# Other starting positions for the low parts of split weights, one for each stretch of the program

## The chip, the core and the metric

The kernel runs on one core of a Trainium2 chip. The metric is the device time of one execution in microseconds (us), as the median of several runs; lower is better. Beside it stands one profiled execution, whose span (first to last instruction) the traces are read against.

## What is computed

The reference is a small encoder of two layers on x (256 positions, 2048 features, float32). Cut to what matters here:

```python
xn = _rmsnorm(x, norm_gain[0])
q, k, v, gate = split(xn @ attn_w_in)          # 2048 x 8192
a = softmax(q1 k1 + bias) - lam * softmax(q2 k2 + bias)
x = x + (norm(a @ v) * silu(gate)) @ attn_w_out    # 2048 x 2048
xn = _rmsnorm(x, norm_gain[1])
a, g, z = split(xn @ conv_w_in + b)            # 2048 x 6144
u = layernorm(depthwise_conv31(a * sigmoid(g)))
x = x + (silu(u) * silu(z)) @ conv_w_out + b   # 2048 x 2048
return _rmsnorm(x, final_gain)
```

Nearly all work is in the four products with weights: 18432 columns of 2048 weights each.

## The kernel before

**The split.** A product of float32 operands is made of three products in float32r, a format that TensorE takes in one pass but rounds. Each operand is split in a high part (rounded) and a low part (the rest), and high times high, high times low and low times high are added up in PSUM.

**The ring of weights.** The weights pass in 144 chunks of 4 x 128 rows by 512 columns (1 MiB), through a ring of four slots. A DMA on SP's queue brings a chunk to `w_raw[slot]`; ScalarE writes the high part to `w_hi[slot]` (`high_part`, L463); VectorE (`low_part`, L807), or GpSimd in the middle of the second layer and for one chunk before it (L435), writes `w_lo[slot]`; TensorE multiplies and counts up `w_free`, which lets ScalarE write the slot again. All four steps of a chunk are released by semaphores.

**Two kinds of chunk.** In a *turned* chunk the weights are the stationary operand and 256 columns of activations stream past them (`project_tile`): 48 matmuls of 128x256 in a chunk, 16 of them with a low part as the stationary operand (L1238, in the first four chunks L1284). Q and K of the attention and all of the conv input are turned: 80 chunks. In a *rows* chunk the activations are stationary and 512 columns of weights stream (`project`): 24 matmuls of 128x512 in a chunk, 8 of them with the low part moving (L1223). V, the gate and both output products are rows: 64 chunks. In the profile's names the moving operand of a matmul stands first and the stationary one second.

**The places in a slot.** Each slot of `w_hi` and `w_lo` is 2048 elements and a gap of `W_GAP` = 128 (8704 bytes, 17 times 512). A chunk's part begins at an offset in its slot, the same for high and low: 0 for a turned chunk, 16 elements for a rows chunk (`place`, L296). Every reader and writer takes its view from `w_part` (L306), with the same chunk number. Within a chunk the pieces lie 512 or 2048 bytes apart. By the program's allocation all slots of `w_hi` and `w_lo` begin 128 bytes past a multiple of 512 bytes in their partition, and the activations (`act_hi`, `act_lo`, `conv_hi`, `conv_lo`) and the small operands q, k, v 192 bytes past one; their own pieces lie multiples of 512 bytes apart. So, modulo 512 bytes, a turned weight lies at 128 and the activations that stream past it at 192; a moving rows weight lies at 192 (128 + 64), as its stationary activations do.

**Order.** The attention runs in four pairs of heads (pair 0, a hardware loop over pairs 1 and 2, pair 3), each with four chunks of Q, K, V and gate. The scores (L1310 to L1312) and the product with V (L1324 to L1326) stand between rows chunks. Then come 16 chunks of output product, 48 turned chunks of the second layer's input, and 16 rows chunks of its output. In the 48, VectorE computes the convolution's taps (L1039), and after each pair of tiles TensorE does four transposes (`v_turn`, L1197) of `uT`, whose rows are 1144 bytes apart.

Of the kernel before, what the change touches and what calls it, by code (L numbers as in the profile page):

```python
# [37 lines left out]
NCH = KT // CK  # L38
# [6 lines left out]
CHUNKS_ATT = 4 * NCH * PAIRS  # L45
CHUNKS_OUT = CHUNKS_ATT + NCH * PAIRS
CHUNKS_CONV = CHUNKS_OUT + 3 * NCH * PAIRS
# [3 lines left out]
VEC_ROOM = 9 * KT + 4  # L51
W_GAP = 128
TURNED_AT, ROWS_AT = 0, 16
WARM_UP = 9
POOL_FROM = CHUNKS_OUT + 2 * RING
POOL_TO = CHUNKS_CONV + RING
# [16 lines left out]
def build(nc, x, x_turned, vectors, taps, final_gain, rel_bias, attn_w_in, attn_w_out, conv_w_in,  # L73
          conv_w_out, conv_b_out, out):
    with ExitStack() as ctx:
        def sb(name, shape, dt=F32, scope=ctx):
            return scope.enter_context(nc.sbuf_tensor("sb_" + name, shape, dt))
# [10 lines left out]
        w_hi = [sb(f"w_hi{i}", [P, CK * GW + W_GAP], F32R) for i in range(RING)]  # L88
# [165 lines left out]
        at = 0  # L254
        for i in range(CONV_START, CONV_END + 1):
            upto = len(STEPS) * (i + 1 - CONV_START) // (CONV_END + 1 - CONV_START)
            steps_at[i] = STEPS[at:upto]
            at = upto
# [37 lines left out]
        def place(c):  # L296

            turned = c % 16 < 2 * NCH if c < CHUNKS_ATT else CHUNKS_OUT <= c < CHUNKS_CONV
            return TURNED_AT if turned else ROWS_AT

        def pair_chunk(j, i):

            in_loop = type(j) is not int
            return 16 * (1 if in_loop else j) + i

        def w_part(parts, c):  # L306

            at = place(c)
            return parts[c % RING][:, at:at + CK * GW].rearrange("p (k n) -> p k n", k=CK)

        def low_part_ready(eng, c):
# [99 lines left out]
        def _(pool):  # L411
# [20 lines left out]
            def low_part(c):  # L432

                pool.wait_ge(hi_ready, c + 1)
                pool.tensor_tensor(w_part(w_lo, c), w_raw[c % RING][:], w_part(w_hi, c).bitcast(F32),  # L435
                                   ALU.subtract).then_inc(lo_ready_pool, 1)
# [22 lines left out]
        def _(act):  # L459
            def high_part(c, slot, loads, like=None):  # L460
                act.wait_ge(landed[slot], 16 * loads)
                act.wait_ge(w_free, c + 1)
                act.activation(w_part(w_hi, c if like is None else like), w_raw[slot][:], ACT.Copy  # L463
                               ).then_inc(hi_ready, 1)
# [14 lines left out]
            for p, (k0, k1) in enumerate(HEAD):  # L479
                slot, rows, closes = head_piece(p)  # L480
                act.wait_ge(x_landed[p], 16)
                for kt in range(k0, k1):
                    act.activation(act_hi[:, kt], xT[:, kt], ACT.Copy, scale=gain_in[:, kt:kt + 1]
                                   ).then_inc(split_hi, 1)
                if p:
                    act.wait_ge(piece_landed(p), 16)
                    act.activation(w_part(w_hi, slot)[:, rows], w_raw[slot][:, rows], ACT.Copy
                                   ).then_inc(hi_ready if closes else head_hi, 1)
# [35 lines left out]
            def pair_slot(j, i):  # L524

                G, A = 4 * j, A_START + A_PER_PAIR * j
                if i in (9, 10):
                    high_part(16 * j + i + RING, i % NCH, 4 * j + i // NCH + 2, pair_chunk(j, i + RING))
                    for hq in ((0, 1) if i == 9 else (2, 3)):
                        act.wait_ge(max_ready, 4 * j + hq + 1)  # L530
                        for c in range(2):
                            act.activation(probs[:, hq, c], probs[:, hq, c], ACT.Exp,
                                           bias=neg_max[:, 2 * hq + c:2 * hq + c + 1],
                                           accum_out=row_sum[:, 2 * hq + c:2 * hq + c + 1]
                                           ).then_inc(exp_done, 1)
                    return
# [34 lines left out]
                if i == 15:  # L571
                    empty_acc(G + 3, 1, g_rows, ACT.Silu, rstd)
                high_part(16 * j + i + RING, i % NCH, 4 * j + i // NCH + 2, pair_chunk(j, i + RING))

            def m_high(n):
# [219 lines left out]
        def _(dve):  # L795
# [61 lines left out]
            def pair_slot(j, i):  # L857
# [84 lines left out]
                if not by_pool(16 * j + i + RING):  # L942
                    low_part(16 * j + i + RING, i % NCH, pair_chunk(j, i + RING))
# [251 lines left out]
        def _(pe):  # L1195
# [133 lines left out]
            pe.wait_ge(consts_ready, 1)  # L1329
            for _ in range(WARM_UP):  # L1330
                pe.matmul(bank_d[0][:, 0:P], ones[:], ones[:], start=True, stop=True)
# [109 lines left out]
```

## Time and profile before

| | |
|---|---|
| median of 3 runs | 842.39 us (841.7 to 846.05) |
| the profiled execution, its own time | 841.85 us |
| its span | 840.1 us |
| TensorE busy | 830.6 us, 5628 matmuls |
| VectorE busy | 646.6 us |
| ScalarE busy | 448.9 us |
| GpSimd busy | 226.4 us |

The profiled execution's time is 1.75 us more than its span (what lies around it), and 0.54 us under the median. Ends of matmuls are modelled in these profiles: a matmul shows a longer duration than the distance to the next one, and the distance is what costs time. It is read from a stretch's length and the number of matmuls in it.

### The profile page before, as it was taken

What the parts mean: (1) busy time and instruction counts of PE and PEld (TensorE: products, weight loads), DVE (VectorE), ACT (ScalarE), POOL (GpSimd) and SP (SyncE); (2) the same over time, 40 slices, a digit from 0 to 9 for tenths busy, and PEclk for the clock granted to TensorE, in tenths of its full rate; (3) what the DMA queues carried; (4) which work ended last, traced back from release to release, by engine and by line L of the source; (5) the groups of instructions that cost most, each with busy time, mean ns of one, the idle gap of its engine ahead of it and who ended that gap; (6) DMA issues with size and microseconds to landing.
All of it is one profiled execution on the core that took longest, in us unless ns stands there. A gap on an engine that the chain in (4) does not pass through costs nothing.

```text
span 840.1 us, 13845 instructions
## 1 busy us (share of the span) xinstructions
PE 830.6 (99%) x5628; PEld 769.4 (92%) x5628; DVE 646.6 (77%) x1097; ACT 448.9 (53%) x589; POOL 226.4 (27%) x107
## 2 busy tenths in 40 slices
PE   9999999999999999999999999999999999999996
PEld 9998899889998899888888999999999999998885
DVE  7569784697658784698788978999999997566651
ACT  7756643646336643556544464454555456594432
POOL 0200000000000000002000008888889877680000
PEclk9999999999999999999999999999999999999998
DMA  9977566546654566534655665555555655549502
GB/s 327 395 275 265 170 200 202 181 139 200 208 192 150 169 199 203 184 117 158 228 181 188 199 211 191 189 171 193 199 163 192 200 173 180 189 163 350 183 18 100
DMA packets 99649, 163.68 MB, mean 195 GB/s; under 512 B 3584, under 2 KB 40704, under 8 KB 99080
## 3 DMA queue, kind: packets, MB, share of 16 engines
q1 hardware_dynamic: 98112, 160.64, 56.4%
q10 hardware_dynamic: 1480, 2.25, 0.7%
q8 instruction: 39, 0.64, 0.3%
q14 instruction: 18, 0.15, 0.1%
HBM read 160.76 MB, written 3.69 MB: 196 GB/s over the span
## 4 chain that ended last, share of the span: by engine, by line
PE 96%; SPq 2%; DMA 1%; ACT 1%; DVE 0%; issue 0%; ACTq 0%
PE ps_acc L1238 17%; PE ps_acc L1237 17%; PE ps_acc L1235 17%; PE ps_acc L1221 14%; PE ps_acc L1223 14%; PE ps_acc L1224 14%; SPq L345 1%; DMA sb_w_raw<-in_attn_w_in 1%; SPq L344 1%; PE ps_d L1312 0%; PE ps_a L1326 0%; PE ps_a L1325 0%; PE ps_d L1311 0%; PE ps_a L1324 0%; PE ps_d L1310 0%; PE ps_a L1197 0%
## 5 line engine op out<-in xcount | busy, mean ns | idle before, releaser
L463 ACT ACTIVATE sb_w_hi<-sb_w_raw 128x2048 fp32r<-128x2048 f32 x140 | 267.1, 1916 | 244.3 <-PE ps_acc L1238 168.2
L435 POOL TENSOR_TENSOR sb_w_lo<-sb_w_raw,sb_w_hi 128x2048 fp32r<-128x2048 f32 x45 | 208.6, 4642 | 404.7 <-ACT sb_w_hi L463 404.7
L807 DVE TENSOR_TENSOR sb_w_lo<-sb_w_raw,sb_w_hi 128x2048 fp32r<-128x2048 f32 x95 | 216.2, 2289 | 98.7 <-ACT sb_w_hi L463 98.3
L1235 PE MATMUL ps_acc<-sb_conv_hi,sb_w_hi 128*128 128x256 f32 x768 | 214.9, 280 | 0.0
L1237 PE MATMUL ps_acc<-sb_conv_lo,sb_w_hi 128*128 128x256 f32 x768 | 213.9, 278 | 0.0
L1238 PE MATMUL ps_acc<-sb_conv_hi,sb_w_lo 128*128 128x256 f32 x768 | 213.7, 278 | 0.0
L1039 DVE SCALAR_TENSOR_TENSOR ps_d<-sb_uT,sb_dwT,ps_d 128x256 f32<-128x256 f32 x480 | 188.9, 481 | 4.5 <-ACT ps_d L688 4.5
L1221 PE MATMUL ps_acc<-sb_w_hi,sb_act_hi 128*128 128x512 f32 x384 | 149.7, 390 | 0.0
L1223 PE MATMUL ps_acc<-sb_w_lo,sb_act_hi 128*128 128x512 f32 x384 | 149.5, 389 | 0.0
L1224 PE MATMUL ps_acc<-sb_w_hi,sb_act_lo 128*128 128x512 f32 x384 | 149.4, 389 | 0.0
L1235 PEld LDWEIGHTS ps_acc<-sb_conv_hi,sb_w_hi 128*128 128x128 f32 x768 | 144.2, 188 | 0.1
L1237 PEld LDWEIGHTS ps_acc<-sb_conv_lo,sb_w_hi 128*128 128x128 f32 x768 | 144.1, 188 | 0.1
L1238 PEld LDWEIGHTS ps_acc<-sb_conv_hi,sb_w_lo 128*128 128x128 f32 x768 | 144.0, 188 | 0.0
L1235 PE MATMUL ps_acc<-sb_act_hi,sb_w_hi 128*128 128x256 f32 x448 | 125.1, 279 | 1.7 <-DVE sb_w_lo L807 1.7
L1238 PE MATMUL ps_acc<-sb_act_hi,sb_w_lo 128*128 128x256 f32 x448 | 125.2, 280 | 0.0
L1237 PE MATMUL ps_acc<-sb_act_lo,sb_w_hi 128*128 128x256 f32 x448 | 124.9, 279 | 0.0
L1224 PEld LDWEIGHTS ps_acc<-sb_w_hi,sb_act_lo 128*128 128x128 f32 x384 | 72.1, 188 | 15.1
L1221 PEld LDWEIGHTS ps_acc<-sb_w_hi,sb_act_hi 128*128 128x128 f32 x384 | 72.1, 188 | 14.8 <-DVE sb_act_lo L973 0.2
L1235 PEld LDWEIGHTS ps_acc<-sb_act_hi,sb_w_hi 128*128 128x128 f32 x448 | 83.8, 187 | 2.0 <-issue 1.9
L1223 PEld LDWEIGHTS ps_acc<-sb_w_lo,sb_act_hi 128*128 128x128 f32 x384 | 72.1, 188 | 14.2
L1237 PEld LDWEIGHTS ps_acc<-sb_act_lo,sb_w_hi 128*128 128x128 f32 x448 | 84.2, 188 | 0.1
L1238 PEld LDWEIGHTS ps_acc<-sb_act_hi,sb_w_lo 128*128 128x128 f32 x448 | 84.1, 188 | 0.0
(168 smaller groups left out, 874.2 us busy)
## 6 DMA issues: line engine op xcount, KB each, us to landing
sb_w_raw<-in_attn_w_in SPq DMA_DIRECT2D x60, 1024.0 KB, 5.6
sb_w_raw<-in_conv_w_in SPq DMA_DIRECT2D x64, 512.0 KB, 4.5
sb_w_raw<-in_attn_w_out SPq DMA_DIRECT2D x16, 1024.0 KB, 5.0
sb_w_raw<-in_conv_w_in SPq DMA_DIRECT2D x16, 1024.0 KB, 5.0
sb_w_raw<-in_conv_w_out SPq DMA_DIRECT2D x16, 1024.0 KB, 5.0
sb_w_raw<-in_attn_w_in SPq DMA_DIRECT2D x16, 256.0 KB, 4.5
sb_xs<-in_x SPq DMA_DIRECT2D x2, 1024.0 KB, 13.9
sb_x_in<-in_x_turned SPq DMA_DIRECT2D x15, 128.0 KB, 4.3
```

What stands on the lines that cost most here:

```text
L344: sp.dma_start(x_piece(x_in, p), x_piece(x_turned, p)).then_inc(x_landed[p], 16)
L345: sp.dma_start(w_raw[slot][:, rows], w_in[:, k0:k1, 0:GW]).then_inc(piece_landed(p), 16)
L435: pool.tensor_tensor(w_part(w_lo, c), w_raw[c % RING][:], w_part(w_hi, c).bitcast(F32), ALU.subtract).then_inc(lo_ready_pool, 1)
L463: act.activation(w_part(w_hi, c if like is None else like), w_raw[slot][:], ACT.Copy).then_inc(hi_ready, 1)
L807: dve.tensor_tensor(w_part(w_lo, like), w_raw[slot][:], w_part(w_hi, like).bitcast(F32), ALU.subtract).then_inc(lo_ready, 1)
L1039: dve.scalar_tensor_tensor(out_, uT[:, k, tap:tap + SEQ], dwT[:, k, tap:tap + 1], out_, ALU.mult, ALU.add).then_inc(tap_done, 1)
L1221: pe.matmul(into, left_hi, high[:, k], start=(kt == 0 and not filled), stop=False, skip_group_check=filled)
L1223: pe.matmul(into, left_hi, low[:, k], start=False, stop=False, skip_group_check=filled)
L1224: ins = pe.matmul(into, left_lo, high[:, k], start=False, stop=(kt == KT - 1), skip_group_check=filled)
L1235: pe.matmul(into, left_hi, hi[:, kt], start=(kt == 0 and f % 2 == 0), stop=False, skip_group_check=True)
L1237: pe.matmul(into, left_hi, lo[:, kt], start=False, stop=False, skip_group_check=True)
L1238: ins = pe.matmul(into, left_lo, hi[:, kt], start=False, stop=(kt == KT - 1), skip_group_check=True)
```

## The change

The low part of a chunk gets its own offset (`low_place`), while the high part keeps the one it had. The offset of the low part, in elements of 4 bytes, depends on the stretch: in turned chunks 16 for pair 0, 32 for Q and K of pairs 1 and 2 and Q of pair 3, 48 for K of pair 3; in rows chunks of the pairs 0, 32, 32 and 48; in the output product 8; in the 48 chunks of the conv input, eight by eight, 16, 32, 48, 8, 4 and 24; in the last output product 24. All lie within the gap that the slots have. Nothing is added, removed or moved in any engine's order; only the views that L435, L807, L839, L1223, L1238 and L1284 write or read differ.

```diff
 TURNED_AT, ROWS_AT = 0, 16
+LOW_TURNED_AT, LOW_ROWS_AT = (16, 32, 32, 48), (0, 32, 32, 48)
+LOW_OUT_AT, LOW_CONV_AT, LOW_CONV_OUT_AT = 8, (16, 32, 48, 8, 4, 24), 24
...
+        def low_place(c):
+
+            if c >= CHUNKS_CONV:
+                return LOW_CONV_OUT_AT
+            if c >= CHUNKS_OUT:
+                return LOW_CONV_AT[(c - CHUNKS_OUT) // (2 * NCH)]
+            if c >= CHUNKS_ATT:
+                return LOW_OUT_AT
+            j, t = c // 16, c % 16 // NCH
+            if t == 0 and j:
+                return LOW_TURNED_AT[1]
+            return LOW_TURNED_AT[j] if t < 2 else LOW_ROWS_AT[j]
...
         def w_part(parts, c):
 
-            at = place(c)
+            at = place(c) if parts is w_hi else low_place(c)
             return parts[c % RING][:, at:at + CK * GW].rearrange("p (k n) -> p k n", k=CK)
```

## Rows read from the trace of the kernel before

**Rows 1.** The page: TensorE's busy time, and its granted clock in 40 slices.

```profile
PE 830.6 (99%) x5628; PEld 769.4 (92%) x5628; DVE 646.6 (77%) x1097; ACT 448.9 (53%) x589; POOL 226.4 (27%) x107
PEclk9999999999999999999999999999999999999998
```

**Rows 2.** The page: the chain that ended last, by engine.

```profile
PE 96%; SPq 2%; DMA 1%; ACT 1%; DVE 0%; issue 0%; ACTq 0%
```

**Rows 3.** Waits: who waited for whom, us, times, longest.

```profile
ACT sb_w_hi L463 <- PE ps_acc L1238: 168.2, 60, 3.9
...
PE ps_acc L1235 <- DVE sb_w_lo L807: 1.7, 1, 1.7
```

**Rows 4.** Windows of turned chunks, L1235 alone (a third of the matmuls), first kind.

```profile
101.90:147.10 45.20, 35.66 (x128) 23.75 (x127) 1.00 0.59 194
...
472.70:546.80 74.10, 58.23 (x208) 38.87 (x207) 1.00 0.63 207
569.40:620.80 51.40, 40.43 (x144) 27.05 (x144) 1.00 0.56 185
648.80:718.00 69.20, 54.02 (x192) 36.07 (x192) 1.00 0.57 186
```

**Rows 5.** The same, second kind: window, length, matmuls and weight loads of L1235.

```profile
30.00:46.30 16.30, 13.28 (x48) 8.99 (x48) 1.00 1.00 373
547.20:569.00 21.80, 17.74 (x64) 12.01 (x64) 1.00 0.57 188
621.20:648.40 27.20, 22.14 (x80) 14.99 (x80) 1.00 0.56 181
718.80:746.10 27.30, 22.24 (x80) 14.96 (x80) 1.00 0.44 150
```

**Rows 6.** Windows of the first four chunks, L1277 alone (a third of the matmuls).

```profile
6.93:22.43 15.50, 6.94 (x44) 5.81 (x44) 1.00 1.05 375
...
24.03:26.75 2.72, 1.23 (x8) 1.05 (x9) 1.00 1.08 413
```

**Rows 7.** A window of the output product, L1221 alone (a third of the matmuls).

```profile
385.60:472.60 87.00, 49.87 (x128) 23.84 (x127) 1.00 0.53 180
```

**Rows 8.** Timeline of TensorE in the scores: start, us, line.

```profile
63.50 0.28 PE L1311 MATMUL ps_d<-sb_k_lo,sb_q_hi 128*128 128x256 f32 x1
...
64.70 0.28 PE L1312 MATMUL ps_d<-sb_k_hi,sb_q_lo 128*128 128x256 f32 x1
```

**Rows 9.** Timeline of TensorE behind the first two groups of transposes.

```profile
547.22 0.36 PE L1235 MATMUL ps_acc<-sb_conv_hi,sb_w_hi 128*128 128x256 f32 x1
547.42 0.28 PE L1237 MATMUL ps_acc<-sb_conv_lo,sb_w_hi 128*128 128x256 f32 x1
...
569.43 0.36 PE L1235 MATMUL ps_acc<-sb_conv_hi,sb_w_hi 128*128 128x256 f32 x1
569.64 0.28 PE L1237 MATMUL ps_acc<-sb_conv_lo,sb_w_hi 128*128 128x256 f32 x1
```

**Rows 10.** Weight loads of the transposes: min, median, max ns.

```profile
L1197 PEld LDWEIGHTS ps_a<-sb_ident,sb_uT x32: 137/140/143, 546.8 to 712.2; 128*128 128x128 f32 x32
```

**Rows 11.** The writers of the low parts: min, median, max ns of one.

```profile
L807 DVE TENSOR_TENSOR sb_w_lo<-sb_w_raw,sb_w_hi x95: 2277/2292/2294, 27.6 to 813.7; 128x2048 fp32r<-128x2048 f32 x95
...
L435 POOL TENSOR_TENSOR sb_w_lo<-sb_w_raw,sb_w_hi x45: 4617/4642/4690, 392.4 to 751.5; 128x2048 fp32r<-128x2048 f32 x45
```

**Rows 12.** A window of VectorE alone, to the end of the convolution's last tap.

```profile
520.00:710.30 190.30, 185.84 (x465) 1.00 0.57 186
```

**Rows 13.** Timeline where the convolution ends: last taps, then ScalarE's copy of them.

```profile
701.65 8.70 DVE L1039 SCALAR_TENSOR_TENSOR ps_d<-sb_uT,sb_dwT,ps_d 128x256 f32<-128x256 f32 x22
...
710.39 0.60 ACT L700 ACTIVATE sb_uT<-ps_d 128x512 f32<-128x512 f32 x1 [1.87 <-DVE ps_d L1039]
```

## The prediction

> **What bounds the kernel now.** I read the page first. TensorE is busy for 830.6 of 840.1 us and its granted clock stands in the highest tenth in all slices but the last [rows 1], which is the 2.4 GHz level. The chain that ended last is 96% TensorE [rows 2]. Then the waits: ScalarE waits 168.2 us for TensorE to free slots, while in the longest stretches TensorE waits for a low part once, for 1.7 us [rows 3]. So the supply of weights runs ahead, and the time is the sum of the distances between matmuls. An offset in SBUF adds no instruction; it can move the time only by changing these distances, or by slowing a writer so much that it falls behind.
>
> So I measured the distances, stretch by stretch, as length over matmuls (three times the count of one line). The turned chunks have two. In the first kind, 101.90 to 147.10 holds 3 x 128 matmuls: 45.2 / 384 = 117.7 ns. The stretches from 472.70, 569.40 and 648.80 give 118.8, 119.0 and 120.1 ns, with the pauses and transposes inside them [rows 4]; the Q and K stretches from 196.4 and 291.0 repeat the first row. In the second kind it is 113.2 ns (16.3 us for 144), 113.5, 113.3 and 113.8 [rows 5]. The first four chunks show both: 117.4 ns over 132 matmuls, then 2.72 us / 24 = 113.3 [rows 6]. Taking 117.78 and 113.33 as the two paces, 62 of the 80 turned chunks go at the slow one and 18 at the quick one. The rows chunks have one pace: 87.0 us / 384 = 226.6 ns [rows 7]. The scores, same shape as a turned matmul, go at (64.70 - 63.50) / 10 = 120 ns [rows 8].
>
> Streaming alone takes 256 / 2.4 GHz = 106.7 ns, or 213.3 for 512 columns. What is on top is 6.7, 11.1 or 13.3 ns. I work with 6.67 ns, the time of 16 columns or 64 bytes, as the quantum: quick turned matmuls have one, the scores and the rows matmuls two, the slow turned ones five in three matmuls.
>
> Do addresses matter to this? Two things speak on it. Chunks, slots and pieces move by multiples of 512 bytes and the pace of a stretch does not move with them, so only the place modulo 512 bytes can count. And scores and turned matmuls have the same shapes and the same order of high and low, but the scores' stationary and moving operands lie at the same place modulo 512 (192 and 192), as those of rows chunks do, while turned ones lie 64 bytes apart (128 and 192). The first two have two quanta everywhere, the turned ones one or one and two thirds. That is the only hint that place matters, and it is a correlation over two distances. Against it: at one and the same distance both turned paces occur, and which one a stretch gets is settled where it begins. After the first group of transposes the second matmul starts 0.20 us after the first and the stretch is quick; after the second group it is 0.21 us and the stretch is slow [rows 9, 5, 4].
>
> **The change part by part.** *The writers.* Every low part is written once more at another offset. VectorE needs 2277 to 2294 ns and GpSimd 4617 to 4690 ns whether the offset is 0 or 16 elements [rows 11]. Offsets 4, 8 and 24 are the first that are no multiple of 64 bytes. GpSimd is the one near a limit: a turned chunk lasts 48 x 117.78 = 5.65 us, so it has 1.0 us left; under 22% more per write costs nothing, and I take nothing for both. Beyond that, each of the 24 chunks of conv input at offsets 8, 4 and 24 would be late by the excess, and TensorE would wait for it.
>
> *Turned chunks, offset 16* (pair 0's Q and K and the first eight of the conv input: 16 chunks, 16 low matmuls each). The low weight comes to lie at 192, like the activations: the distance of the scores. Nearest row: 120 ns. 256 matmuls x 2.22 ns = +0.57 us. If the whole stretch goes to 120 from what it has, it is 12 x 48 x 2.22 + 4 x 48 x 6.67 = +2.6 us; if it goes to the quick pace, 12 x 0.213 = -2.6 us.
>
> *Turned chunks, offsets 32 and 48* (28 and 12 chunks). The low weight lies 64 and 128 bytes behind the activations; no row shows these distances. Bounds for a chunk: from 117.78 to 113.33, -0.213 us; to 120, +0.107 us. The high parts, two thirds of the loads, stay where they are, and I expect the stretch to keep its pace: 0.
>
> *Turned chunks, offsets 8, 4, 24* (24 chunks of the conv input). A stationary operand at no multiple of 64 bytes is shown by the transposes, whose tiles lie at steps of 1144 bytes: all 32 loads take 137 to 143 ns [rows 10]. So 0, with the same bounds.
>
> *Rows chunks.* In 16 (pairs 1 and 2, offset 32) the moving low weight gets 64 bytes away from the stationary operand, as in turned chunks; one matmul in three could have 2.2 ns less: 128 x 2.22 = -0.28 us. Pairs 0 and 3 (offsets 0 and 48): 0. The 32 chunks of the two output products (8 and 24) have a moving row of 2048 bytes that begins in the middle of 64 bytes and so touches 33 of them, not 32. A quantum for each would be 256 x 6.67 = +1.7 us, nothing if it hides in the two quanta already paid; no row decides, and I take half, +0.85 us. Bounds for all 512 low rows matmuls: a quantum less or more, -3.4 to +3.4 us.
>
> A rule of the Trainium skill speaks against any effect. SBUF — State Buffer, section "SBUF: two separate sides", has TensorE on ports of its own, with "2nd independent read port for LDWEIGHTS", and places its banks along partitions, not along a partition. By it the whole edit is worth 0 and the time is that of before; the rows neither confirm nor exclude it. TensorE: Matmul & The Clock Gate, section "Wait — 56ns, not 53.3ns?", gives streaming plus about 2.5 ns for a matmul, an estimate of 109.2 ns here; the rows disagree (113.3 to 120), so something is lost that this page does not explain.
>
> *Sum.* +0.57 - 0.28 + 0.85 = +1.1 us. On the profiled execution, 841.85 us (span 840.1 and 1.75 around it), it gives 842.95; on the median, 0.54 us higher, 843.5.
>
> **The rivals.**
>
> *Faster: the low parts release the slow pace.* If the slow pace is a lock between two equal streams, moving one load in three can break it. All 62 slow chunks at 113.33: 62 x 48 x 4.44 = -13.2 us, so 829.2 us; with half of it, 835.8. For it: the quick pace exists with the same instructions [rows 5]. Against: two thirds of the loads don't move. It would be given back in part in the second layer: VectorE has only 190.3 - 185.84 = 4.5 us idle up to its last tap [rows 12], and ScalarE's copy ends at 710.99 us [rows 13], about 1.0 us before the last four transposes, whose last load starts at 712.2 [rows 10], against 5.3 us that 25 slow chunks there would save. The cap of some 5.5 us just about lets it pass. I put it at 829 to 838.
>
> *Slower: every turned chunk goes at the pace of the scores.* One conflicting load in three upsets the other two, and the pace becomes 120 ns: 62 x 48 x 2.22 + 18 x 48 x 6.67 = 6.6 + 5.8 = +12.4 us, 854.8 us; with half, 848.6. Losing the quick stretches alone to 117.78 is 18 x 0.213 = +3.8 us. It decides against the kernel from 4.2 us, which a third of this sum reaches. For it: the only distances in the trace show equality as dearer, and unequal places of high and low put a jump into a stream that had none. With a quantum for each of the 512 rows matmuls too, 858.
>
> *Slower: a moving operand pays for the jump itself.* In rows chunks the stream goes high, low, high at one place now; if each jump costs a quantum, two in a triple, it is 512 x 2 x 6.67 = +6.8 us, 849.2 us. For it, rows chunks are so regular; against, turned ones don't change moving places and yet vary.
>
> *No effect of place at all*: 842.4, by the two separate reads. It falls together with my forecast. The draw of slow and quick stretches can still differ: one stretch of five chunks is 5 x 0.213 = 1.1 us.
>
> **How the numbers follow.** About 0.5%, 4.2 us, is what a measurement of this kernel can tell from no change. Chances: the forecast with the rival of no effect 0.38, near 843.5 (its own range 839 to 846.5, three or four stretches that change pace); the release 0.28, at 829 to 838; turned chunks at the scores' pace 0.24, at 847 to 855; the jump in rows 0.10, at 847 to 851. So faster 0.28, same 0.38, slower 0.34. The range is from 831, which leaves out the full release, to 855, the full loss.
>
> **What the profile after would show.** The distances by stretch: 113.3, 117.8 or 120 ns in the turned stretches, 226.7 or more in rows, above all in the output products with offsets 8 and 24. A distance outside these (say 115.6, or 240 and more) would say that place acts more strongly than by one quantum, and would make the sum wrong. The durations of L807 and L435 should stay at 2.29 and 4.64 us; waits of TensorE for L435 would mean that a writer suffers from the offset. If in one stretch the pace follows the offset and in none the beginning, place matters; if all stretches show the paces of before, it doesn't.

## The result and the profile after

The changed kernel takes 846.27 us (845.93 to 847.36, 10 runs) against 842.53 for the kernel before (10 runs): ratio 1.0044, 95% interval 1.0035 to 1.0052. It is slower by 2.9 to 4.4 us, less than 0.5% but clear of the noise. The forecast was a change within 0.5%, near 843.5 us, with an own range of 839 to 846.5: the measured time lies 2.8 us above the number and inside the range. Its profiled execution took 846.21 us (span 844.4), 4.36 more than the one of before.

The page after, busy times and granted clock, beside [rows 1]:

```profile
PE 835.2 (99%) x5628; PEld 767.5 (91%) x5628; DVE 646.2 (77%) x1097; ACT 449.2 (53%) x589; POOL 226.3 (27%) x107
PEclk9999999999999999999999999999999999999999
```

The same 5628 matmuls at the same clock keep TensorE busy 4.6 us longer. The writers did not change, whatever the offset (L822 and L450 are L807 and L435 of before, [rows 11]):

```profile
L822 DVE TENSOR_TENSOR sb_w_lo<-sb_w_raw,sb_w_hi x95: 2281/2291/2297, 27.1 to 817.6; 128x2048 fp32r<-128x2048 f32 x95
...
L450 POOL TENSOR_TENSOR sb_w_lo<-sb_w_raw,sb_w_hi x45: 4608/4634/4720, 392.6 to 753.1; 128x2048 fp32r<-128x2048 f32 x45
```

TensorE has no wait for either writer in the second layer. So it is the distance between matmuls again. Windows of rows chunks after, L1236 alone (a third of the matmuls; columns as in [rows 4]): three adjacent chunks each of pairs 0, 1 and 3, then the two output products.

```profile
77.54:94.04 16.50, 9.36 (x24) 4.32 (x23) 1.00 0.47 152
173.17:189.85 16.68, 9.45 (x24) 4.32 (x23) 1.00 0.46 149
361.13:377.78 16.65, 9.44 (x24) 4.31 (x23) 1.00 0.36 126
386.18:474.94 88.76, 49.99 (x128) 23.94 (x127) 1.00 0.53 182
748.62:832.03 83.41, 47.27 (x121) 22.61 (x121) 1.00 0.50 175
```

Length over three times the count: 229.2 ns with the low part at 0, 231.7 at 32, 231.3 at 48, 231.1 at 8, and 231.7 at 24 (83.41 us for the 15 chunks of 24 matmuls that end there). Before, all were at 226.7 [rows 7]. Every new offset made rows chunks dearer.

Windows of turned chunks after, L1250 alone: pair 1 and pair 2 (Q and K, offset 32), K of pair 3 (48), four chunks of the conv input (32) and its last four (24):

```profile
102.39:148.00 45.61, 35.72 (x128) 23.84 (x127) 1.00 0.57 190
198.32:241.80 43.48, 35.33 (x128) 23.84 (x127) 1.00 0.59 196
...
313.88:336.10 22.22, 17.85 (x64) 11.86 (x64) 1.00 0.67 224
...
520.60:542.36 21.76, 17.66 (x65) 12.01 (x65) 1.00 0.58 192
...
726.01:748.60 22.59, 17.92 (x64) 11.90 (x64) 1.00 0.46 152
```

All 24 chunks at 8, 4 and 24 ran at 117.7 to 118.0. Offset 32 gives 118.8 ns in pair 1 (45.61 / 384) and 113.2 in pair 2; 48 gives 115.7 (K of pair 3); the conv input has 21.76 / 192 = 113.3 at 32 and 117.7 at 24 in its last four chunks, which ran at 113.3 before. (A window's count can be one off at its ends; chunks are exact: 48 matmuls in each.) Summed over all matmuls by the distance to the next one, the rows stretches have 6.5 us more, the turned ones 2.0 us less and the rest 0.1 less: +4.4, the whole difference of the two executions.

### The profile page after: what moved, and what is told of

It is laid out like the page before. It is cut to its first block, busy times and chain, and to the rows that moved or that the text cites. A ratio compares the mean times of both kernels' runs of the same rounds, so it can differ in the third digit from the quotient of the medians.

```text
span 844.4 us, 13845 instructions
## 1 busy us (share of the span) xinstructions
PE 835.2 (99%) x5628; PEld 767.5 (91%) x5628; DVE 646.2 (77%) x1097; ACT 449.2 (53%) x589; POOL 226.3 (27%) x107
## 4 chain that ended last, share of the span: by engine, by line
PE 96%; SPq 2%; DMA 1%; ACT 1%; DVE 0%; issue 0%; ACTq 0%
PE ps_acc L1252 17%; PE ps_acc L1250 17%; PE ps_acc L1253 17%; PE ps_acc L1238 14%; PE ps_acc L1239 14%; PE ps_acc L1236 14%; SPq L360 1%; DMA sb_w_raw<-in_attn_w_in 1%; SPq L359 1%; PE ps_a L1341 0%; PE ps_a L1339 0%; PE ps_a L1340 0%; PE ps_d L1326 0%; PE ps_d L1327 0%; PE ps_d L1325 0%; PE ps_a L1212 0%
## 5 line engine op out<-in xcount | busy, mean ns | idle before, releaser
L450 POOL TENSOR_TENSOR sb_w_lo<-sb_w_raw,sb_w_hi 128x2048 fp32r<-128x2048 f32 x45 | 208.8, 4644 | 404.7 <-ACT sb_w_hi L478 404.7
L822 DVE TENSOR_TENSOR sb_w_lo<-sb_w_raw,sb_w_hi 128x2048 fp32r<-128x2048 f32 x95 | 216.1, 2290 | 101.5 <-ACT sb_w_hi L478 101.1
L1250 PE MATMUL ps_acc<-sb_conv_hi,sb_w_hi 128*128 128x256 f32 x768 | 214.9, 280 | 0.0
L1238 PE MATMUL ps_acc<-sb_w_lo,sb_act_hi 128*128 128x512 f32 x384 | 151.4, 394 | 0.0
L1239 PE MATMUL ps_acc<-sb_w_hi,sb_act_lo 128*128 128x512 f32 x384 | 151.1, 394 | 0.0
L1236 PE MATMUL ps_acc<-sb_w_hi,sb_act_hi 128*128 128x512 f32 x384 | 150.6, 392 | 0.0
L1250 PEld LDWEIGHTS ps_acc<-sb_conv_hi,sb_w_hi 128*128 128x128 f32 x768 | 144.3, 188 | 0.1
L1250 PE MATMUL ps_acc<-sb_act_hi,sb_w_hi 128*128 128x256 f32 x448 | 124.7, 278 | 1.4 <-DVE sb_w_lo L822 1.4
L1236 PEld LDWEIGHTS ps_acc<-sb_w_hi,sb_act_hi 128*128 128x128 f32 x384 | 72.2, 188 | 16.1
L1238 PEld LDWEIGHTS ps_acc<-sb_w_lo,sb_act_hi 128*128 128x128 f32 x384 | 72.1, 188 | 16.0
L1250 PEld LDWEIGHTS ps_acc<-sb_act_hi,sb_w_hi 128*128 128x128 f32 x448 | 84.1, 188 | 1.8 <-issue 1.6
```

The lines of the kernel that those rows point to most:

```text
L822: dve.tensor_tensor(w_part(w_lo, like), w_raw[slot][:], w_part(w_hi, like).bitcast(F32), ALU.subtract).then_inc(lo_ready, 1)
L1236: pe.matmul(into, left_hi, high[:, k], start=(kt == 0 and not filled), stop=False, skip_group_check=filled)
L1238: pe.matmul(into, left_hi, low[:, k], start=False, stop=False, skip_group_check=filled)
L1239: ins = pe.matmul(into, left_lo, high[:, k], start=False, stop=(kt == KT - 1), skip_group_check=filled)
L1250: pe.matmul(into, left_hi, hi[:, kt], start=(kt == 0 and f % 2 == 0), stop=False, skip_group_check=True)
```

## The experiments

All are the kernel before with other offsets. `place` takes them from two tables, for high and low parts, in the order of pair 0, pairs 1 and 2 (with Q of pair 3), pair 3, and the quarters of an output product or the twelve groups of four chunks of the conv input:

```diff
-        def place(c):
+        def place(c, part):
...
+            if c >= CHUNKS_CONV:
+                return ROWS[part][2][(c - CHUNKS_CONV) // NCH]
+            if c >= CHUNKS_OUT:
+                return TURNED[part][1][(c - CHUNKS_OUT) // NCH]
+            if c >= CHUNKS_ATT:
+                return ROWS[part][1][(c - CHUNKS_ATT) // NCH]
...
-            at = place(c)
+            at = place(c, 'hi' if parts is w_hi else 'lo')
```

In the profiles of these kernels L1231 and L1245 are L1221 and L1235 of before. "Alike" means high and low at the same offset.

**1. The rows' half alone.**

```diff
-ROWS low:  16 everywhere
+ROWS low:  0 | 32 | 48, output products 8 and 24
```

> The change in the rows chunks alone; low parts of turned chunks at 0 as before. If the place of a low part acts in its own chunks and nowhere else, the rows stretches show the distances of the changed kernel (229 to 232 ns) and give +6.5 us, with the turned stretches as before up to a redraw of their pace of 1 to 3 us: 847 to 851 us. If the dearer rows came from something shared (writers, the change of offset between stretches), they would be partly back at 226.7 ns and the time under 845.

844.62 us (10 runs; the kernel before beside it 842.59), ratio 1.0023 (1.0014 to 1.0033). Two windows of L1231, pair 1 and the first output product, then two of L1245, three chunks of K of pair 0 and Q and K of pair 2:

```profile
172.85:189.53 16.68, 9.45 (x24) 4.32 (x23) 1.00 0.47 149
385.42:474.17 88.75, 49.99 (x128) 23.91 (x127) 1.00 0.54 183
...
29.63:46.59 16.96, 13.46 (x48) 8.94 (x48) 1.00 1.01 375
198.01:241.53 43.52, 35.33 (x128) 23.84 (x127) 1.00 0.59 195
```

The two rows windows are those of the changed kernel to 0.01 us, and the rows stretches have +6.3 us in sum. (The last output product, at 24 in both, ran at 231.1 ns here and at 231.7 there: rows stretches can differ at one offset too.) But the turned chunks, in which nothing was edited, gained 3.6 us: pairs 2 and 3 went from 117.7 to 43.52 / 384 = 113.3 ns. The time came out 2.4 us under the expected range. By itself it would have fitted the rival of something shared (under 845); the distances of the rows, dearer throughout, refute that. So a turned stretch's pace hangs on more than its own offsets. Not only on the rows before it, either: K of pair 0, which runs before any rows chunk, went from 113.2 ns [rows 5] to 16.96 / 144 = 117.8.

**2. The turned half alone.**

```diff
-TURNED low:  0 everywhere
+TURNED low:  16 | 32 | 48, conv input 16, 32, 48, 8, 4, 24 (eight chunks each)
```

> The change in the turned chunks alone; low parts of rows chunks at 16 as before. Same theory: rows at 226.7 ns everywhere, turned at 113.3 ns where the low offset is 32, 115.6 where it is 48, 117.8 elsewhere: -2 us to -4 us, 838 to 841. Rival, that the pace of a turned stretch is drawn by how it begins and not by the offset: the paces by stretch then come in another order than in the changed kernel, 838 to 846.

838.02 us (4 runs), ratio 0.9944 (0.9924 to 0.9963). Windows of L1245, pair 1, K of pair 3 and the conv input at 32:

```profile
102.27:145.81 43.54, 35.33 (x128) 23.84 (x127) 1.00 0.62 204
309.82:331.98 22.16, 17.86 (x64) 11.87 (x64) 1.00 0.68 228
514.40:536.16 21.76, 17.66 (x64) 12.01 (x65) 1.00 0.59 192
```

Rows are at 226.7 again, turned chunks 4.0 us cheaper than before. Paces by offset are those of the changed kernel, except that pair 1 now has the quick one, 113.4 ns, at the same offset that gave 118.8 there. The change was two edits of opposite sign, and they don't add up: the halves alone are +2.0 and -4.6 us against the kernel before, -2.5 in sum, and the whole is +3.7. The rows' cost is the same with and without the other half (6.3 and 6.5 us); what differs are the turned chunks, 3.6 and 4.0 us cheaper in the halves and only 2.0 in the whole.

**3 and 4. Offset 32 in all turned chunks, low alone, and alike.**

```diff
-TURNED low:  0 everywhere
+TURNED low:  32 everywhere          (3: high 0, 4: high 32)
```

> Low parts at 32 in all turned chunks, rows as before. If offset 32 brings the quick pace, 62 slow chunks go from 117.78 to 113.33 ns: -13.2 us, 829 to 830. In the changed kernel Q and K of pair 1 ran at 118.9 ns at this offset; if the offset only makes the quick pace likelier, some stretches stay at 118 to 119: 831 to 840. If the pace is only drawn, 842 or so.

> High and low parts both at 32 in all turned chunks, rows as before. If what counts is where a stationary weight lies against the activations that stream (64 bytes ahead before, 64 bytes behind at 32), all three loads have now the place that only the low one had: the quick pace everywhere, 829 to 832. If it is the difference between high and low, there is none, as in the kernel before: paces mixed, 838 to 846.

Low alone: 837.39 us (6 runs), ratio 0.9946 (0.9926 to 0.9967). Alike: 839.80 us (7 runs), ratio 0.9959 (0.9945 to 0.9973). Two windows of L1245 of the first, pair 1 and three chunks of the conv input, then two of the second:

```profile
102.60:146.20 43.60, 35.33 (x128) 23.84 (x127) 1.00 0.61 200
546.60:563.70 17.10, 13.38 (x48) 8.89 (x48) 1.00 0.57 185
```

```profile
102.00:147.20 45.20, 35.97 (x128) 23.84 (x127) 1.00 0.59 197
...
655.70:672.00 16.30, 13.20 (x48) 8.85 (x48) 1.00 0.54 175
```

Low alone has 113.5 and 118.8 ns (17.10 / 144) and, behind the first three chunks, never 117.8. Alike has 117.7 and 113.2, as the kernel before, though the weights lie on the other side of the activations. Part of the first run's rival is what happened: the offset makes the quick pace likelier, and some stretches stay at 118 to 119 (831 to 840 us). "32 makes it quick" fell; so did my theory for the second run, that this side of the activations is the better one. What fits is that an offset sets which paces a stretch can have.

**5. Rows, high and low alike at other offsets.**

```diff
-ROWS high, low:  16 everywhere
+ROWS high, low:  0 | 32 | 48, first output product 0, 32, 64, 96, last 8, 24, 4, 16
```

> Turned chunks as before; in the rows chunks high and low parts lie at the same offset, but at another one in each stretch: 0, 32 and 48 in the pairs, 0, 32, 64 and 96 in the four quarters of the first output product, 8, 24, 4 and 16 in those of the last. If the difference between high and low makes rows dear, there is none: 226.7 ns everywhere, and 842 +- 2 us. If the place against the stationary activations does, 229 to 232 ns as in the changed kernel, 849. If a row that begins at no multiple of 64 bytes costs by itself, only 8, 24 and 4 are dearer (+2 us or so).

849.03 us (2 runs), ratio 1.0074 (1.0054 to 1.0094). L1231 in the four quarters of the first output product, then in those of the last (its last window holds three chunks of 24 matmuls):

```profile
389.24:411.64 22.40, 12.65 (x33) 6.02 (x32) 1.00 0.40 131
411.64:433.61 21.97, 12.42 (x32) 6.01 (x32) 1.00 0.60 216
433.61:456.00 22.39, 12.65 (x32) 6.02 (x32) 1.00 0.54 188
456.00:477.98 21.98, 12.42 (x32) 5.82 (x31) 1.00 0.59 191
751.20:773.61 22.41, 12.66 (x33) 6.09 (x33) 1.00 0.80 299
773.61:796.01 22.40, 12.64 (x33) 6.00 (x32) 1.00 0.66 227
796.01:818.53 22.52, 12.69 (x32) 6.03 (x32) 1.00 0.28 94
818.53:834.87 16.34, 9.34 (x25) 4.50 (x24) 1.00 0.14 54
```

By 96 matmuls to a quarter: 233.3, 228.9, 233.2, 229.0 ns, 233.4 at offset 8, 233.3 at 24, 234.6 at 4, and 226.9 at 16 in the end. Offset 32 has a second pace here: 228.9 ns in pair 1, but 233.3 from the second half of V of pair 2 to the end of that pair (16.80 / 72 in 268.38 to 285.18). No low part lies elsewhere than its high part, and all but 16 is dearer. The rival of the prediction that a jump of the moving stream costs is refuted as the cause: there is no jump in this run. And 64 equals 0, 96 equals 32: the period is 256 bytes, not only 512. Whether a row begins at a multiple of 64 bytes doesn't decide: 0 is as dear as 8. Offset 4 is the dearest of all by 1.3 ns; why, no run tells.

**6. A survey of differences between high and low.**

```diff
-TURNED low:  0 everywhere;  ROWS high, low:  16 everywhere
+TURNED low:  64 | 128 | 96 in the pairs, conv input 128, 64, 96, 112 (three groups each)
+ROWS high:  16 | 0 | 16, 16 16 16 0, 64 32 16 16;  low:  80 | 128 | 112, 0 32 80 128, 0 0 24 16
```

> A survey of differences low minus high, in elements. Turned: 64 for pair 0, 128 for pairs 1 and 2 and Q of pair 3, 96 for K of pair 3, and 128, 64, 96, 112 for three groups each of the conv input. Rows: 64, 128, 96 in the pairs, -16, 16, 64, 128 in the quarters of the first output product, -64, -32, 8, 0 in those of the last. If only the difference modulo 512 bytes counts, 128 equals 0: rows at 226.7 ns, turned at 113.3 or 117.8. If a smaller period holds (256 bytes), 64 is like 0 too. If the difference as such costs, 128 is as dear as 16 or 32 (229 to 232 ns). Time not forecast; the distances by stretch are what counts.

850.31 us (1 run). L1231 in three chunks of pair 0 (16 and 80), of pair 1 (0 and 128), and in the third and fourth quarter of the first output product (16 and 80, 0 and 128):

```profile
77.97:94.29 16.32, 9.34 (x24) 4.32 (x23) 1.00 0.49 154
173.13:189.93 16.80, 9.46 (x24) 4.31 (x23) 1.00 0.46 149
...
434.39:456.18 21.79, 12.47 (x33) 6.01 (x32) 1.00 0.55 190
456.18:478.57 22.39, 12.62 (x32) 5.80 (x31) 1.00 0.58 191
```

and L1245 in K of pair 3 (low at 96) and three of the last four chunks of the conv input (low at 112):

```profile
316.79:339.61 22.82, 17.88 (x64) 11.90 (x64) 1.00 0.62 205
...
730.98:747.62 16.64, 13.41 (x49) 8.99 (x49) 1.00 0.44 149
```

A low part 256 bytes behind the high one's place costs nothing (226.7 and 227.0 ns), and 512 bytes behind offset 0 it is as dear as 0 alike (233.3 and 233.2). So both of my cases for 128 failed as stated: the difference is without effect, but the base of it wasn't 226.7. In turned chunks 64 and 128 ran at 117.8, the slow pace of 0; 96 at 118.9 (four chunks of 16 at 113.3), as 32 did, and 112 at 115.6 (16.64 / 144), as 48 did. So the period of 256 bytes shows in turned chunks as well.

**7. The activations moved by 64 bytes, with rows alike.**

```diff
-        o_stat = sb("o_stat", [P, 16])
+        o_stat = sb("o_stat", [P, 32])[:, 0:16]
-ROWS high, low:  16 everywhere
+ROWS high, low:  16 | 32 | 48, first output product 32, 16, 0, 80, last 32
```

> All activations moved by 64 bytes (o_stat made 16 elements longer), turned weights at 0 as before, rows at 16 in pair 0, 32 in pairs 1 and 2, 48 in pair 3; 32, 16, 0, 80 in the quarters of the first output product and 32 in the last, high and low alike. If the distance between weights and activations counts: 226.7 ns at 32, where they are together again, 233.3 at 16 and 80, 229 or 233 at 48, and turned chunks as with 48 everywhere. If the place of the weights by itself counts: 226.7 at 16 and 80, 229 at 32, 233.3 at 0, turned chunks as before.

853.72 us (1 run). L1231 in three chunks each of pair 0 (16) and pair 1 (32), in two quarters of the first output product (32, 16) and in 15 chunks of the last (32); then L1245 in pair 2, offset 0:

```profile
78.94:95.74 16.80, 9.46 (x24) 4.31 (x23) 1.00 0.46 149
174.49:190.81 16.32, 9.34 (x24) 4.32 (x23) 1.00 0.48 153
...
390.46:412.23 21.77, 12.46 (x32) 6.01 (x32) 1.00 0.38 126
412.23:434.63 22.40, 12.61 (x32) 5.99 (x32) 1.00 0.64 223
...
758.00:839.63 81.63, 46.71 (x120) 22.61 (x121) 1.00 0.50 178
```

```profile
199.16:245.24 46.08, 36.01 (x128) 24.18 (x127) 1.00 0.57 191
```

This decides it. With the activations 64 bytes further, 32 is the offset at 226.7 ns (22.4 / 96 = 233.3 at 16), and the turned chunks, whose weights were not moved, went to 120.0 in pairs 0, 2 and 3 and to 118.7 in pair 1 and most of the conv input. Those are the paces of run 8, in which the weights are moved instead and lie at the same distance, 128 bytes. The place of the weights by itself does not set the pace; its distance to the other operand, modulo 256 bytes, does.

**8 and 9. Turned chunks alike at other distances.**

```diff
-TURNED high, low:  0 everywhere
+TURNED high, low:  48 everywhere                                       (8)
+TURNED high, low:  16 | 16 | 64, conv input 16, 48, 8, 96 (three groups each)   (9)
```

> High and low parts of all turned chunks at 48, rows at 16 as before. In byte places modulo 256 the stationary weights then lie at 64 and the activations that stream at 192, as far from each other as they can be. If the distance between the two operands' places sets the pace and the greatest one is the best for turned chunks, 113.3 ns everywhere: 829 to 831 us. If it acts only in rows chunks, where it was seen, the paces stay mixed between 113.3 and 117.8: 838 to 843.

> A survey with high and low at the same offset in turned chunks: 16 for pairs 0 to 2 and Q of pair 3, 64 for K of pair 3; three groups each of 16, 48, 8 and 96 in the conv input. If the distance of the two operands counts, 16 (no distance) gives the 120 ns of the scores, 64 what 0 gave, 96 what 32 gave, 48 the same as the kernel with 48 everywhere. If turned chunks don't care for it, 113.3 or 117.8 at each of them.

The first: 851.02 us (4 runs), ratio 1.0098 (1.0082 to 1.0115). The second: 847.45 us (1 run). L1245 in pair 1 of the first:

```profile
104.74:150.83 46.09, 35.97 (x128) 24.13 (x127) 1.00 0.59 193
```

and, in the second, in pair 1 (16), twice two chunks at 8, and four at 96:

```profile
104.23:150.30 46.07, 36.22 (x128) 24.38 (x127) 1.00 0.58 194
...
615.92:627.23 11.31, 8.99 (x32) 5.89 (x32) 1.00 0.59 187
...
633.28:644.48 11.20, 8.93 (x33) 6.01 (x33) 1.00 0.58 186
...
684.62:706.40 21.78, 17.67 (x64) 11.90 (x64) 1.00 0.57 186
```

The greatest distance, 128 bytes, was to be the best if distance mattered, and was among the worst: 120.0 ns in pairs 1 to 3 and 118.6 to 118.8 in pair 0 and most of the conv input, some 20 us above the forecast. Distance matters, but not in that way. Equality (16) gives the 120.0 of the scores in all chunks that had it, as expected; offset 8, 32 bytes apart, gave 117.8 (11.31 / 96) or 116.7; 64 and 96, 64 bytes to either side, gave 113.3 (0 and 32, at the same two distances, have 117.8 too).

**10. Offset 48 where 32 had run at 118.9.**

```diff
-TURNED low:  0 everywhere
+TURNED low:  48 | 32 | 32, conv input 32 32 32 48 48 32 32 32 48 48 48 48
```

> Rows as before; low parts of turned chunks at 32, but at 48 in pair 0 and in those parts of the conv input where the kernel with 32 everywhere ran at 118.9 ns. At 48 both kernels that had it ran at 115.6 ns whatever stood before. If that holds, 27 or so chunks have 3.3 ns less per matmul than with 32 everywhere, -4 us: 833 to 835. If the pace after a pause is redrawn by any edit, 834 to 839.

836.65 us (4 runs), ratio 0.9924 (0.9907 to 0.9940). The chunks at 48 in the conv input ran at 115.6 ns, as forecast; but the start of the conv input, still at 32, fell from 113.3 to 118.9. It came out above the expected 833 to 835 and inside the 834 to 839 of its rival, a pace redrawn by any edit.

**11 and 12. Two tables from what was seen.**

```diff
-TURNED low:  0 everywhere
+TURNED low:  32 | 32 | 32, conv input 32 32 32, 48 48 48, 32 32, 96 x4   (11)
+TURNED low:  32 | 32 | 32, conv input 32 32 32, 96 x9                    (12)
+TURNED high: 96 where low is 96, else 0
```

> Rows at 16 throughout. Turned chunks: high 0 and low 32 in the pairs and in the first three groups of the conv input, low 48 in groups 3 to 5 (12 chunks), low 32 in 6 and 7, high and low both at 96 in the last four. If a distance sets which paces a stretch can have and the stretches keep those seen (113.3 at 32 from its start, 115.6 at 48, 113.3 at 96 behind other places), the kernel with 32 everywhere loses 9 x 0.16 and some 14 x 0.27 us: 831 to 833 us. If the pace is drawn anew after each pause, some of the last sixteen chunks run at 117.8: 833 to 837.

> As the other, but high and low both at 96 in all conv groups from the fourth. With 32 and 32, the same distance to the activations, the first half of the conv input ran mostly at 117.8 and the second mostly at 113.3. If that is a draw at each pause, not a matter of place, some of these 36 chunks run at 117.8, others at 113.3: 832 to 838 us; all at the quick pace: 829 to 831.

832.40 us (5 runs), ratio 0.9884 (0.9868 to 0.9900), and 833.80 us (4 runs), ratio 0.9892 (0.9877 to 0.9908). The first fell in the range of stretches that keep their paces, the second in that of a draw, and both beat the kernel before and the changed one. L1245 in the eight chunks from the fifth of the conv input, the first kernel and the second:

```profile
491.21:534.73 43.52, 35.33 (x129) 24.03 (x129) 1.00 0.70 228
```

```profile
492.06:537.71 45.65, 35.71 (x129) 24.02 (x129) 1.00 0.67 219
```

Up to here the two kernels are the same in every offset and every instruction. One runs these chunks at 113.3 ns, the other at 118.9; the two executions differ in the waits ahead of them, by a microsecond or so. The paces part in the fourth chunk of the conv input, behind a pause in which TensorE waits 0.6 us for VectorE (L1036) and does two matmuls that belong to no chunk (L1262). So at one distance the pace of a stretch is drawn where it begins, between two fixed values.

## Why the prediction was right, and where it was not

**The bound and the measure** held: TensorE's chain, the writers at unchanged duration, no new wait, and all of the difference in the distances between matmuls. The prediction's own sign that place acts more strongly than by one quantum, a distance such as 115.6 ns, came true in the 12 chunks at offset 48.

**"Only the place modulo 512 bytes can count", and that the distance between the operands matters**, was offered as a correlation over two distances. Run 7 shows it, with the period halved to 256 bytes (runs 5 and 6). The reading of it was wrong in one half: for turned chunks equality is dear (120.0), for rows chunks it is the only cheap place of those tried (226.7). The two are different: at the same distance a stream of 512 columns and one of 256 are not hurt alike.

**The rows chunks** were the mis-sized term. For offset 32 I took -0.28 us, by the turned pace; it measured 16 chunks x 24 x (231.7 - 226.7) = +1.9. For 0 and 48 I took 0 without a row for it, though offset 0 puts the two operands 64 bytes apart just as 32 does; they gave +1.1, by the sums over their stretches. For the output products I took half a quantum for each low matmul, +0.85; they gave +3.5 (some 384 x 4.4 and 384 x 5.0 ns), two quanta and more in each group of three, and not because of rows beginning within 64 bytes. In sum 6.5, against +0.6 forecast. The bound of +3.4 us was too narrow too: 6.5 us are 12.6 ns for each of the 512 matmuls that were moved, nearly two quanta.

**The turned chunks** were forecast at +0.57 and gave -2.0 us. Offset 32, taken as 0, brought the quick pace to 20 of its 28 chunks and 118.9 to the other 8, -3.2 us; 48 a pace of its own, 115.6, -1.0 us. Offset 16, the only one with a term, +0.57, gave +0.1: its chunks after the first four ran at 117.8, not nearer to 120. The offsets 8, 4 and 24, taken as 0, held all their chunks at 117.8, ten of which had been quick: +2.1 us. Part of this is not the offset's doing, as run 1 shows.

**The sum** came near by luck: two errors of opposite sign, 5.9 us too little for the rows and 2.6 us too much for the turned chunks, left 3.3. The change that was measured is more than three times the +1.1 us that was forecast. The range and the class held for the same reason: rival cases of opposite sign each happened in a part of the program.

**The rivals.** The release happened at offset 32, in 20 of the 80 turned chunks, 17 of them slow before. The pace of the scores appeared at distance 0 in run 9 and at 128 bytes in runs 7 and 8, where turned chunks cost 8.8 us more (run 8); not in the changed kernel, where only one part in three was moved. The jump is refuted by run 5. "No effect of place" is refuted by runs 5, 7 and 8. The Trainium skill, SBUF — State Buffer, "SBUF: two separate sides", from which the prediction took this rival, gives LDWEIGHTS a read port of its own, independent of the moving operand's. No run here tells which ports there are; but weight loads and moving operands of one TensorE are not independent of each other's places, by run 7.

What stays open is the mechanism: why 256 bytes, why equality helps one shape and hurts the other, and what decides the draw at a stretch's start. Turned and rows chunks differ in more than the columns of a matmul: in one the weights are stationary, in the other they stream, and no run takes the two apart. The scores, with 256 columns and other operands, speak for the columns: 120.0 at distance 0. That the draw also differs between executions of one kernel is argued only: the profiled execution of run 12, 836.75 us, is the slowest of its four, 2.7 us above the next. The nine chunks at 118.9 instead of 113.3 would make 9 x 48 x 5.6 ns = 2.4 us of it, an estimate. The others were not profiled.

## What to carry to other kernels

When TensorE bounds a kernel and its matmuls are dense, measure the distance between matmuls by stretch before anything else: some nanoseconds over streaming, times thousands, are a place to look. In float32r the places of stationary and moving operand modulo 256 bytes are a knob: a few unused elements before a tensor turn it, the writers here took no longer for it, and a survey with another offset in each stretch reads many settings in one run. Judge such a survey by its stretches and not by its total, and expect settings to be good for one shape alone; repeat what is chosen, since a stretch's pace can be drawn between two values where it begins.

## What the runs showed of the hardware

Distance of the weights' place behind the activations' modulo 256 bytes, and the time between matmuls, high and low alike:

| bytes | 512 columns moving, ns | 256 columns moving, ns |
|---|---|---|
| 0 | 226.7 | 120.0 |
| 32 | 233.3 | |
| 64 | 228.9 or 233.3 | 113.3 or 117.8 |
| 128 | 232.1 to 232.8 | 118.7 or 120.0 |
| 192 (64 before) | 233.3 | 113.3 or 117.8 |
| 208 (48 before) | 234.6 | |
| 224 (32 before) | 233.3 | 116.7 or 117.8 |

An empty field was not measured. The weights are the moving operand in the first column of times and the stationary one in the second. Streaming alone, taken as in the prediction at the 2.4 GHz level, is 213.3 and 106.7 ns, so the overhead runs from 6.7 to 21.3 ns. A pace is constant over hundreds of matmuls while VectorE, ScalarE, GpSimd and DMAs come and go, which argues that it belongs to TensorE's own two streams. With high and low at different places further paces appear (115.6, 118.9; 231.1, 231.7).
